# Output projection of a hybrid decoder step: six column pairs by seven block products of 132 tokens in place of eight

## What is computed

```
cat = jnp.concatenate([o.reshape(b, t, ATT_WIDTH), y_conv], axis=-1)
return cat @ w_out
```

## Time and profile before

| what | value |
|---|---|
| median of 3 runs | 1437.7 us (1435.02 to 1438.22) |
| the profiled execution | 1436.35 us |
| its span, first to last instruction | 1434.4 us |
| mean granted TensorE clock | 0.947 |
| TensorE matmul busy | 1242.1 us (87%), 8998 instructions |
| weight loads busy | 675.9 us (47%) |
| VectorE busy | 433.2 us (30%) |
| ScalarE busy | 217.4 us (15%) |
| GpSimd busy | 45.4 us (3%) |
| moved by DMA | 503.63 MB, 351 GB/s over the span |

### The profile page before, as it was taken

One profiled execution on the slowest core, in us unless ns is written; L12 is line 12 of the kernel. 1 busy time (PEld: TensorE's weight loads), 2 busy tenths in 40 slices (PEclk: granted clock), 3 DMA queues, 4 the chain that ended last, 5 costly groups with the idle time before them and its releaser, 6 DMA issues.

```text
span 1434.4 us, 21171 instructions
## 1 busy us (share of the span) xinstructions
PE 1242.1 (87%) x8998; PEld 675.9 (47%) x8998; DVE 433.2 (30%) x863; ACT 217.4 (15%) x462; POOL 45.4 (3%) x33
## 2 busy tenths in 40 slices
PE   9999999999999998997877778796787787777887
PEld 8888888888788862331222232132232122213223
DVE  4322127674211143322311321231222231132142
ACT  3111232322000043110101111011011010101101
POOL 0000003140000001000000000000000000000000
PEclk9999999999999999998989998899999898999899
DMA  9975443669399359999999999999999999999997
GB/s 342 348 227 183 140 133 121 206 206 340 88 349 413 121 182 427 417 425 435 427 433 432 430 433 431 431 431 431 431 432 432 430 432 432 432 432 430 433 426 317
DMA packets 101202, 503.63 MB, mean 351 GB/s; under 512 B 9294, under 2 KB 79638, under 8 KB 86182
## 3 DMA queue, kind: packets, MB, share of 16 engines
q1 hardware_dynamic: 89346, 494.86, 85.0%
q10 hardware_dynamic: 11812, 8.14, 1.8%
HBM read 496.42 MB, written 6.59 MB: 351 GB/s over the span
## 4 chain that ended last, share of the span: by engine, by line
PE 53%; DMA 44%; DVE 2%; ACT 1%; issue 0%; DVEq 0%; ACTq 0%; SPq 0%
PE bank L735 31%; DMA ring<-in_w_gate 16%; DMA ring<-in_w_up 15%; DMA ring<-in_w_down 12%; PE bank L1023 9%; PE bank L1058 3%; PE bank L958 2%; PE bank L1076 1%; DVE xa L1913 1%; PE bank L1073 1%; DMA xa<-in_x_prompt 1%; PE bank L746 0%; PE bank L826 0%; PE bank L776 0%; PE bank L1084 0%
## 5 line engine op out<-in xcount | busy, mean ns | idle before, releaser
L1023 PE MATMUL bank<-ring,bc 128*32 128x512 f32 x2040 | 272.4, 669 | 113.7 <-DMA ring<-in_w_gate 61.9
L735 PE MATMUL bank<-bc,ring 128*128 128x264 f32 x1536 | 350.8, 387 | 1.3 <-ACT cat L1261 1.3
L735 PEld LDWEIGHTS bank<-bc,ring 128*128 128x128 f32 x1536 | 288.2, 190 | 51.5 <-issue 2.3
L1023 PEld LDWEIGHTS bank<-ring,bc 128*32 128x32 f32 x2040 | 63.7, 118 | 288.2 <-issue 146.5
L1913 DVE TENSOR_TENSOR xa<-xa,bank 128x512 f32<-128x512 f32 x128 | 79.3, 682 | 153.0 <-PE bank L1076 146.6
L735 PE MATMUL bank<-cat,ring 128*128 128x264 f32 x512 | 114.9, 387 | 0.0
L735 PEld LDWEIGHTS bank<-cat,ring 128*128 128x128 f32 x512 | 97.0, 190 | 17.7 <-issue 1.3
L1927 DVE COPY bc<-bank 128x512 f32<-128x512 f32 x32 | 22.1, 691 | 234.6 <-PE bank L1023 234.6
L1058 PE MATMUL bank<-ring,cat 128*32 128x512 f32 x480 | 67.2, 684 | 22.4 <-DMA ring<-in_w_down 22.4
L958 PE MATMUL bank<-cat,bc 128*32 128x512 f32 x512 | 61.3, 597 | 13.5 <-DVE xa L1913 13.5
L1487 ACT ACTIVATE bc<-bank 128x512 f32<-128x512 f32 x32 | 19.1, 597 | 289.6 <-PE bank L1023 289.6
(11 more groups left out here) (300 smaller groups left out, 1023.5 us busy)
## 6 DMA issues: line engine op xcount, KB each, us to landing
ring<-in_w_gate SPq DMA_DIRECT2D x27, 4096.0 KB, 31.8
ring<-in_w_up SPq DMA_DIRECT2D x27, 4096.0 KB, 31.6
ring<-in_w_down SPq DMA_DIRECT2D x26, 4096.0 KB, 32.7
ring<-in_w_in SPq DMA_DIRECT2D x23, 2048.0 KB, 15.3
ring<-in_w_up SPq DMA_DIRECT2D x10, 2048.0 KB, 12.9
ring<-in_w_gate SPq DMA_DIRECT2D x9, 2048.0 KB, 15.4
ring<-in_w_down SPq DMA_DIRECT2D x9, 2048.0 KB, 16.1
ring<-in_w_out SPq DMA_DIRECT2D x8, 2048.0 KB, 16.5
```

Of the source, the lines that this page charges most:

```text
L735: m = pe.matmul(bank[n % 3][:, 0:T], w[:, k, (i % TPU) * P:(i % TPU + 1) * P], src[:, k, :], start=n_k == 0, stop=n_k == KT - 1)
L1023: m = pe.matmul(bank[b][c * C:(c + 1) * C, :], xeT[j % 2][:, k, :], wx, start=i == 0 and x < 4, stop=i == 1 and x >= 4, skip_group_check=True)
```

## The change

Tiles 0 to 3 stay as they are (PLAIN = 2 units). The last six units are computed by Strassen's scheme in Winograd's form: cat is split into heads and convolution channels and into tokens 0 to 131 and 132 to 263, W's unit into four quarters of 1024 x 128. Seven products of eight matmuls each (128x128 weights, 132 tokens) stand in place of two tiles of 16 matmuls with 264 tokens. VectorE makes four sums of weights per unit, written into the slot of the unit two before it (T1, T2, T4) or in place (T3), sums of the rows of cat once, and seven additions into `yT` per unit, three banks being shared by the products. The slot of unit u is released when unit u+2 is done, for the last two when they are done themselves. The warm-up at the start becomes 37 matmuls of 48x48. The two clears of VectorE move behind the projection, GpSimd's clear to the projection's end.

```
+PLAIN = 2
+HT = T // 2
+KH = KT // 2
+PRODUCTS = ("P1", "P5", "P2", "P6", "P3", "P7", "P4")
...
+            if kind == "W":
+                last = min(u + PLAIN, KT // 2 - 1) if u + PLAIN < KT // 2 else u
+                eng.wait_ge(product_done, NPROD * (last - PLAIN + 1))
...
-            for _ in range(13):
-                pe.matmul(bank[7][:, 0:P], cold, cold, start=True, stop=True)
+            for _ in range(37):
+                pe.matmul(bank[7][0:48, 0:48], cold[:, 0:48], cold[:, 0:48], start=True, stop=True)
...
+            def product(i, name, rows, weights, to, start, end):
+
+                for k in range(KH):
+                    m = pe.matmul(bank[to][:, 0:HT], weights[:, k, :], rows[k], start=start and k == 0, stop=end and k == KH - 1,
+                                  skip_group_check=True)
+                m.then_inc(product_done, 1)
...
+                product(i, "P1", A11, w["B11"], Y_A, True, False)
...
+                product(i, "P5", S1, w["T1"], Y_B, True, False)
...
+                product(i, "P2", A12, w["B21"], Y_C, True, True)
+                added("P1")
+                summed_weights("T2")
...
+                product(i, "P6", S2, w["T2"], Y_A, False, False)
+                added("P5")
...
+                product(i, "P3", S4, w["B22"], Y_B, False, True)
+                added("P6")
...
+                product(i, "P7", S3, w["T3"], Y_A, False, True)
+                added("P2")
+                summed_weights("T4")
+                product(i, "P4", A22, w["T4"], Y_C, True, True)
...
-            for j in range(KT):
+            for j in range(2 * PLAIN):
                 tile(TILE_AT[("W", j)])
-                if j >= EG and j % EG == 0:
-                    for x in range(j - EG, j):
+            for i in range(PLAIN, KT // 2):
+                two_tiles(i)
+                if i % 2 == 0:
+                    for x in range(2 * (i - 2), 2 * i):
                         router_products(x)
...
+                x, y = {"T1": ("B12", "B11"), "T3": ("B22", "B12"), "T2": ("B22", "T1"), "T4": ("B21", "T2")}[name]
+                V.tensor_tensor(w[name], w[x], w[y], ALU.subtract).then_inc(weight_sums, 1)
...
+                add_product(i, "P1", yT[:, even, lo], a)
+                sum_weights(i + 1, "T1")
+                add_product(i, "P5", yT[:, odd, hi], b)
+                sum_weights(i + 1, "T3")
+                add_product(i, "P2", yT[:, even, lo], c)
+                sum_weights(i + 1, "T2")
+                add_product(i, "P6", yT[:, odd, lo], a)
+                for n in range(max(2 * i - 2, 2 * PLAIN - 1), 2 * i):
+                    add_squares(n)
+                add_product(i, "P3", yT[:, odd, lo], b)
+                sum_weights(i + 1, "T4")
+                add_product(i, "P7", yT[:, even:even + 2, hi], a.unsqueeze(1).to_broadcast([P, 2, HT]))
+                if odd == KT - 1:
+                    add_squares(KT - 2)
+                add_product(i, "P4", yT[:, even, hi], c)
+            st.add(V.memset(logits, FAR))
+            st.add(V.memset(both4, 0.0))
...
-            pool.wait_ge(o_ready, H + 1)
+            pool.wait_ge(product_done, ALL_PRODUCTS)
             G.memset(xa[:, 2, 0:512], 0.0).then_inc(x2_zero, 1)
```

More of the change, by code:

```diff
@@ L141 @@
 NY = 12
+PLAIN = 2
+HT = T // 2
+KH = KT // 2
+Y_TILES = [*range(2 * PLAIN)] + [2 * i + x for i in range(PLAIN, KT // 2) for x in (1, 0)]
+PRODUCTS = ("P1", "P5", "P2", "P6", "P3", "P7", "P4")
+PRODUCT = {p: n + 1 for n, p in enumerate(PRODUCTS)}
+SUMS = ("T1", "T3", "T2", "T4")
+SUM = {p: n + 1 for n, p in enumerate(SUMS)}
+NPROD = len(PRODUCTS)
+ALL_PRODUCTS = NPROD * (KT // 2 - PLAIN)
+Y_A, Y_B, Y_C = ((NIN + 1 + x) % 3 for x in range(3))
 X0_BANKS = (3, 4, 5, 6)
@@ L207, in build @@
         ident = const("ident")
+        lo, hi = slice(0, HT), slice(HT, T)
+        heads, convs = slice(0, KH), slice(KH, KT)
+        A11, A12 = [cat[:, heads, lo][:, k] for k in range(KH)], [cat[:, convs, lo][:, k] for k in range(KH)]
+        A22 = [cat[:, convs, hi][:, k] for k in range(KH)]
+        S3 = [cat[:, heads, hi][:, k] for k in range(KH)]
         hT = bc[:, 0:KT * T].rearrange("p (k t) -> p k t", t=T)
@@ L407, in build @@
         y_copied = sem("y_copied")
+        row_sums = sem("row_sums")
+        weight_sums = sem("weight_sums")
+        product_done = sem("product_done")
+        product_added = sem("product_added")
         y_squared = sem("y_squared")
@@ L484, in arrived, with quarters, y_wait @@
             eng.wait_ge(slot_full[s], value)
+        def quarters(u):
+            w = ring[:, front_at[("W", u)][0], :].rearrange("p (k c) -> p k c", k=KT)
+            to = ring[:, front_at[("W", u - PLAIN)][0], :].rearrange("p (x k c) -> p x k c", x=4, c=P)
+            return {"B11": w[:, 0:KH, 0:P], "B12": w[:, 0:KH, P:], "B21": w[:, KH:, 0:P], "B22": w[:, KH:, P:],
+                    "T1": to[:, 0], "T2": to[:, 1], "T4": to[:, 2], "T3": w[:, 0:KH, P:]}
+        def y_wait(eng, n):
+            if n < 2 * PLAIN:
+                eng.wait_ge(y_copied, n + 1)
+            else:
+                i, x = divmod(n, 2)
+                eng.wait_ge(product_added, NPROD * (i - PLAIN) + PRODUCT[("P7", "P4")[x]])
         def used_wait(eng, n):
             kind, u = FRONT[n]
-            if kind == "KP":
+            if kind == "W":
+                last = min(u + PLAIN, KT // 2 - 1) if u + PLAIN < KT // 2 else u
+                eng.wait_ge(product_done, NPROD * (last - PLAIN + 1))
+            elif kind == "KP":
                 eng.wait_ge(page_sum, PPU * (u + 1))
@@ L877, in router_products @@
                 c = j % EG
-                pe.matmul(bank[6][c * C:(c + 1) * C, 0:T], wrv[:, j, :], yT[:, j, :], start=j < EG, stop=j >= KT - EG,
+                pe.matmul(bank[6][c * C:(c + 1) * C, 0:T], wrv[:, j, :], yT[:, j, :], start=n < EG, stop=n >= KT - EG,
                           skip_group_check=True).then_inc(router, 1)
@@ L1422, in _ @@
             act.dma_start(consts[:, late0:late0 + 512], ins["late"]).then_inc(late_in, 16)
[L1424 to L1428, removed]
+            for n, j in enumerate(Y_TILES):
+                y_wait(act, n)
+                if n >= 3:
+                    act.wait_ge(sq_added, n - 2)
+                A(sqy[n % 2] if n else sacc, yT[:, j, :], ACT.Square).then_inc(y_squared, 1)
             act.wait_ge(sums2, 2)
@@ L1747, in _, with add_squares, sum_rows, sum_weights @@
             dve.wait_ge(s_whole, 1)
-            st.add(V.memset(logits, FAR))
-            st.add(V.memset(both4, 0.0))
             st.add(V.memset(rms, 1.0))
[L1752 to L1759, removed]
+            def add_squares(n):
+                dve.wait_ge(y_squared, n + 1)
+                if n >= 2:
+                    dve.wait_ge(sq_added, n - 1)
+                V.tensor_tensor(sacc, sacc, sqy[n % 2], ALU.add).then_inc(sq_added, 1)
+            def sum_rows(to, x, y, op):
+                V.tensor_tensor(to, x, y, op).then_inc(row_sums, 1)
+            def sum_weights(u, name):
+                if u >= KT // 2:
+                    return
+                w, base = quarters(u), len(SUMS) * (u - PLAIN)
+                if name == "T1":
+                    arrived(dve, ("W", u))
+                    if u - PLAIN >= PLAIN:
+                        dve.wait_ge(product_done, NPROD * (u - 2 * PLAIN + 1))
+                else:
+                    dve.wait_ge(weight_sums, base + SUM["T2" if name == "T4" else "T1"])
+                x, y = {"T1": ("B12", "B11"), "T3": ("B22", "B12"), "T2": ("B22", "T1"), "T4": ("B21", "T2")}[name]
+                V.tensor_tensor(w[name], w[x], w[y], ALU.subtract).then_inc(weight_sums, 1)
+            for j in range(2 * PLAIN):
                 n = TILE_AT[("W", j)]
@@ L1766, in _, with add_product @@
                 V.tensor_tensor(yT[:, j, :], yT[:, j, :], bank[n % 3][:, 0:T], ALU.add).then_inc(y_copied, 1)
+                if j == 0:
+                    dve.wait_ge(o_ready, H + 1)
+                    sum_rows(s1, cat[:, heads, hi], cat[:, convs, hi], ALU.add)
+                    dve.wait_ge(row_sums, 1)
+                    sum_rows(s2, s1, cat[:, heads, lo], ALU.subtract)
+                if j == 1:
+                    for name in SUMS:
+                        sum_weights(PLAIN, name)
+                    dve.wait_ge(row_sums, 2)
+                    sum_rows(s4, cat[:, KH:KT - 1, lo], s2[:, 0:KH - 1], ALU.subtract)
+                    sum_rows(s4_last, cat[:, KT - 1, lo], s2[:, KH - 1], ALU.subtract)
+                if j == 2 * PLAIN - 1:
+                    sum_rows(cat[:, heads, hi], cat[:, heads, lo], cat[:, heads, hi], ALU.subtract)
+            def add_product(i, name, to, src):
+                base = NPROD * (i - PLAIN)
+                dve.wait_ge(product_done, base + PRODUCT[name])
+                earlier = {"P2": "P1", "P3": "P6", "P7": "P5", "P4": "P7"}.get(name)
+                if earlier:
+                    dve.wait_ge(product_added, base + PRODUCT[earlier])
```

(6 more changed lines are left out.)

42 lines of the change are left out of this document (39 added, 3 removed).

## The result

The changed kernel takes 1426.83 us (median of four, 1424.82 to 1429.52) against 1437.12 for the kernel before beside it: ratio 0.9931, 95% interval 0.9919 to 0.9944. The forecast was 1428.2, in a range from 1425.0 to 1433.5.

What follows compares the result with a forecast made beforehand. It took TensorE's matmuls to bound the projection and weight loads the experts, an earlier projection end being kept throughout. Terms -9.5 - 0.13 + 0.1, about -9.5 us, took the median 1437.7 to 1428.2, range 1425 to 1433.5.

Steps and rivals of the forecast that it cites:

- TensorE's part: Projection: 384 matmul steps of 222.5 ns (85.4 us) give way to 672 of 113 ns (75.9 us), gaining 9.5 us.
- The boundaries of the products at 0: Projection: the waits at the start of each product cost TensorE nothing; upper end 2.7 us.
- The estimate of 163 ns a step: Projection: by the skill page's ratio, 672 instructions would take 110 us, making the change a loss of 24 us.
- VectorE at nothing: Projection: VectorE's sums and additions, 7.9 us per unit, hide beside 12.7 us of TensorE and cost nothing.
- the point that the prediction called the tightest: Projection: P7's addition ends at 11.3 us of a unit, needed by the next P1 at 12.7, leaving 1.4 us.
- each microsecond beyond the cover is paid in every unit: Projection: if VectorE's work outgrows TensorE's cover, each microsecond beyond it costs six.
- SP's queue: Projection's end: three slots open together about 507.3; 9.7 us of loads move behind it into 10.9 us of room.
- The start: Kernel start: the smaller warm-up ends near 7.3 us, 0.6 later, mostly hidden by a wait; 0.1 us added.
- a cold start: Kernel start: the small warm-up fails to lift the clock, costing up to 2.8 us, 1431; chance 12%.
- Weight loads uncovered: Projection: each of the 672 steps lasts the recorded weight load, 190 ns, 127.7 us in all, giving 1479.9; chance 5%.
- VectorE late: Projection: sums of weights three times slower, a unit of 17.5 us, +19.6 us; chance 2%.
- The last loads take it back: Behind the projection: 9.7 us of loads find no room and cancel the gain, leaving 1437.9; chance 6%.

Runs made afterwards that it cites:

- doubled sums: Changed kernel with each sum of weights of units 3 to 7 preceded by one more of the same size into an unused quarter; 1431.96 us.
- tripled one: Changed kernel with two more sums of weights ahead of each one in units 3 to 7; 1464.58 us.
- fifth experiment: Changed kernel with the loads of expert units 2 to 7 all waiting for the projection's end, six there in place of three; 1441.74 us.
- ninth run: The changed kernel timed once more, unaltered; 1428.62 us against 1437.32 for the kernel before, ratio 0.9940.
- kernel with seven units: Changed kernel with seven of eight units by Strassen's scheme (PLAIN = 1); 1435.41 us, ratio 0.9987 to the kernel before.
- kernel with seven units, placed: Kernel with seven units, with 30 warm-up matmuls of 60 columns in place of 37 of 48; 1425.48 us, ratio 0.9921 to the kernel before.

## Why the prediction was right, and what it missed

**TensorE's part: right.** The step taken was 113 ns. The chain has 12.60 + 25.40 + 25.40 + 12.80 = 76.2 us for 672 instructions, 113.4 ns, against 75.9 forecast and bounds of 74.9 and 77.1. The gain by steps is 85.4 - 76.2 = 9.2. The projection itself is shorter by 9.85 us (116.47 to 106.62): the other 0.6 is in the steps removed. Behind each of the three router's groups a piece of the chain is some 0.2 us longer than its steps (21.56 for three tiles of 7.12, 12.80 for 12.60), and 85.4, worked out from tiles between two groups, leaves this out, where 76.2 holds it. The boundaries of the products at 0 were right; the upper end of 2.7 was not needed. The reason holds as well: with 100 columns the step is 111.4 ns, so the weight loads set the pace. The estimate of 163 ns a step, worked out there from the figures of the Trainium skill, page "TensorE: Matmul & The Clock Gate", section "Back-to-back issue gap", is not borne out: no piece of the products shows more than 114.3.

**VectorE at nothing: right.** No wait for it within a unit, and VectorE itself still waits 0.20 us or more before each addition of the first unit. The point that the prediction called the tightest, P7's addition, ends some 1.2 us before the next P1 needs it (1.4 reckoned). The doubled sums show the room's end: 4.6 us. The forecast that each microsecond beyond the cover is paid in every unit was good for the doubled kernel (0.6 us of wait in each of five) and too low for the tripled one, since it left out the granted clock.

**SP's queue: right.** Three units together, and room for them. The three loads added in the fifth experiment found hardly any.

**The start: the size off, and its meaning missed.** The term was +0.1. The warm-up ended at 5.77 instead of 7.3, as its steps became shorter within it, and the first tile began at 13.49 (ninth run) and 13.67 where it began at 13.85. So at the first tile the term was between -0.4 and -0.2 in these two. But in nine of eleven profiled executions with a small warm-up the fallen clock or the late load described above made it 0.9 to 1.7 by the projection's first tile; only the two with the clock are a late form of the rival *a cold start*, and the late load was not reckoned with. What the step missed is the code: it looked at the edit of the warm-up for its own time only. With the old warm-up the change gains 2.2 us (1435.15 against 1437.35, one execution each and within their spread), and with 25 matmuls nothing. The change adds 686 instructions ahead of the loop and happens to put it in a good place; the 24 more matmuls of the warm-up are part of that. That the change may cost some 10 us by moving the loop in the code was a rival that was not listed, and no row that the prediction rests on bears on it. Its sum came out right by its steps, and the total came out right also because this rival did not occur, which was luck.

**The other rivals.** *Weight loads uncovered* and *VectorE late* fall by the rows above. *The last loads take it back* falls by the shift of 10.33 us at the loop's first load, against 9.5 reckoned.

**A slip that changes nothing.** The prediction counts its slices of the earlier trace rows too high by one: 121 and 182 stand in the 14th and 15th of the 40, 466 to 538 us, which are the times it means.

## What to carry to other kernels

When the free size falls to where a matmul takes as long as the load of its weights, count instructions, and price them by a traced run whose weights are loaded in the same way; columns saved below that bring next to nothing (here a quarter of them brought 1% of a step). Give each step that moves to another engine a room in microseconds, and test it by doubling that step. Where an engine runs a long loop, read the number of code blocks in the profile's row of instruction queues before and after any edit to that engine's program, even a few instructions far ahead of the loop.

## What the runs showed of the hardware

TensorE's loop here is 6.51 blocks of 16 KB. In some places it is loaded once and stays (33 or 36 blocks in all); in others about nine blocks are loaded in each pass, and TensorE stands for up to 6.8 us at a time at its head (the kernel with seven units). A shift of 28 instructions (30.34 to 30.23) decided 10 us of 1425. Within a straight run of code no such wait was seen: in the projection the blocks of code come in while TensorE runs without a gap.

The Trainium skill, page "Runtime: NRT & Kernel Launch", section "Instruction fetch mechanics", describes instruction memory as a first-in first-out store refilled in blocks of 16 KiB, 128 KiB of it for TensorE, and says that a taken branch to a target outside the window forces a fetch. The runs agree in the size of a block and in the cost at the branch. They show besides that a loop of more than two blocks can stay loaded whole: the ninth run loads no block after 719 us, when the first of the loop's passes is about over (723.47). A simple reading would be that the loop stays if it lies in seven blocks and not if it touches eight, provided that 0.15 to 0.21 of a block of code that the count leaves out stands ahead of the whole program; this would fit all eight places in the table. It is an estimate from the table and was not tested by itself.

The second surprise is the tripled sums: TensorE's five waits of 4.4 us for VectorE came with a mean granted clock of 0.85 over 115 us, and cost 12 us more than the waits alone were expected to.

The kernel with seven units, placed, is the shortest that ran: 1425.48 us. It is shorter than the kernel before by its interval; against the changed kernel the intervals overlap (0.9908 to 0.9935 and 0.9926 to 0.9953), and the spans of the profiled executions differ by 0.4 us (1423.7 and 1424.1).
